# A hybrid diffusion layer on one core: x and positions loaded inside the Fourier stage, its closing barrier split by channel block, and the first choices' rows counted apart

## The reference

```
xl = x + grid_sincos(T, D)
h  = rms_norm(xl, g1) * (1 + scale1) + shift1
y  = sigmoid(g_a) * GLA(h) + sigmoid(g_b) * fourier_mix(h) @ fnet_proj + sigmoid(g_c) * SSD(h)
xl = xl + gate1 * (y @ w_out)
h2 = rms_norm(xl, g2) * (1 + scale2) + shift2
scores = sigmoid(h2 @ router_w)          # 16 experts in 4 groups; best group, then its top 2
xl = xl + gate2 * sum over 2 experts of weight_e * ((silu(h2 @ w1[e]) * (h2 @ w3[e])) @ w2[e])
out = rms_norm(xl, final_g)
```

## Time and profile before

| | us |
|---|---|
| median of 3 runs | 1905.43 (1902.82 to 1907.98) |
| the profiled execution, own time | 1910.72 |
| its span in the profile | 1909.1 |
| PE busy | 1687.8 (88%) |
| DVE busy | 728.6 (38%) |
| ACT busy | 374.4 (20%) |
| POOL busy | 278.9 (15%) |
| mean granted TensorE clock, as a share of full speed | 0.951 |

### The profile page before, as it was taken

One profiled execution on the slowest core, in us unless ns is written; L12 is line 12 of the kernel. 1 busy time (PEld: TensorE's weight loads), 2 busy tenths in 40 slices (PEclk: granted clock), 3 DMA queues, 4 the chain that ended last, 5 costly groups with the idle time before them and its releaser, 6 DMA issues.

```text
span 1909.1 us, 22819 instructions
## 1 busy us (share of the span) xinstructions
PE 1687.8 (88%) x8856; PEld 900.1 (47%) x8857; DVE 728.6 (38%) x1292; ACT 374.4 (20%) x722; POOL 278.9 (15%) x300
## 2 busy tenths in 40 slices
PE   3989799899889889999999999999999867999893
PEld 0554455355355344544454555444656343555441
DVE  1144743754564464620014776214015221222124
ACT  2321232132122122000012333410010121111112
POOL 0003411430530341000000000000000012222122
PEclk9999899999899989999999999999989878999997
DMA  9621101021011116622111001213331645997994
GB/s 314 247 76 44 45 22 45 1 67 44 1 45 45 44 45 220 220 88 89 45 44 44 30 14 45 89 44 104 143 122 45 263 177 205 394 347 291 394 378 152
DMA packets 109537, 242.00 MB, mean 127 GB/s; under 512 B 8505, under 2 KB 18238, under 8 KB 109474
## 3 DMA queue, kind: packets, MB, share of 16 engines
q1 hardware_dynamic: 86800, 180.60, 26.3%
q0 software_dynamic: 14128, 48.51, 7.0%
q10 hardware_dynamic: 8546, 12.03, 1.8%
HBM read 219.10 MB, written 22.02 MB: 126 GB/s over the span
## 4 chain that ended last, share of the span: by engine, by line
PE 75%; DVE 12%; ACT 3%; DMA 3%; issue 3%; POOL 2%; ACTq 2%; DVEq 0%; POOLq 0%; PEldq 0%
PE psum L432 15%; PE psum L1036 8%; PE psum L444 7%; PE psum L722 6%; PE psum L609 4%; PE psum L1058 4%; PE psum L436 4%; PE psum L837 3%; PE psum L667 2%; PE psum L635 2%; PE psum L506 2%; PE psum L454 2%; PE psum L871 1%; PE psum L769 1%; DVE arena L1726 1%
## 5 line engine op out<-in xcount | busy, mean ns | idle before, releaser
L432 PE MATMUL psum<-arena 128*128 128x512 f32 x688 | 312.9, 611 | 10.3 <-issue 4.6
L432 PEld LDWEIGHTS psum<-arena 128*128 128x128 f32 x688 | 132.3, 196 | 171.1 <-issue 163.3
L1036 PE MATMUL psum<-arena 128*32 128x256 f32 x2816 | 166.9, 389 | 1.5 <-DVE arena L2080 1.5
L444 PE MATMUL psum<-arena 128*128 128x512 f32 x352 | 155.2, 600 | 0.1
L609 PE MATMUL psum<-arena 128*128 128x512 f32 x256 | 131.7, 645 | 1.2 <-ACT arena L1230 1.2
L1036 PEld LDWEIGHTS psum<-arena 128*32 128x32 f32 x2816 | 92.2, 111 | 61.2 <-issue 8.5
L722 PE MATMUL psum<-arena 128*128 128x512 f32 x256 | 111.5, 593 | 0.0
L444 PEld LDWEIGHTS psum<-arena 128*128 128x128 f32 x352 | 67.3, 193 | 82.3 <-issue 82.2
L2156 POOL TENSOR_TENSOR arena<-arena 128x512 f32<-128x512 f32 x40 | 49.5, 1248 | 356.5 <-ACT arena L1285 305.6
L2192 POOL TENSOR_TENSOR arena<-arena 128x512 f32<-128x512 f32 x64 | 82.7, 1296 | 101.7 <-ACT arena L1325 101.7
L1682 DVE SCALAR_TENSOR_TENSOR arena<-arena 128x772 f32<-128x772 f32 (+1 forms) x96 | 93.9, 978 | 3.4
(11 more groups left out here) (350 smaller groups left out, 2124.7 us busy)
## 6 DMA issues: line engine op xcount, KB each, us to landing
arena<-exp_w_d SPq DMA_DIRECT2D x48, 2048.0 KB, 17.7
arena<-w_in_d SPq DMA_DIRECT2D x22, 2048.0 KB, 7.9
arena<-ada_w_d POOLq DMA_DIRECT2D x8, 2048.0 KB, 9.1
slots<-arena POOLq DMA_DIRECT2D x1, 9216.0 KB, 27.2
arena<-ada_w_d SPq DMA_DIRECT2D x4, 2048.0 KB, 23.2
arena<-ssd_proj_d SPq DMA_DIRECT2D x4, 2048.0 KB, 9.5
slots<-arena POOLq DMA_DIRECT2D x92, 64.0 KB, 5.0
arena<-slots POOLq DMA_DIRECT2D x22, 256.0 KB, 6.1
```

Source lines behind the costliest of these rows:

```text
L432: ins = mmul(ps[:, 0:T], slot[:, k, m * P:(m + 1) * P], src[:, k, C:NT], start=(k == 0), stop=(k == KD - 1))
L444: ins = mmul(ps[:, 0:n], src[:, k, t * P:(t + 1) * P], slot[:, k, 0:n], start=(k == 0), stop=(k == KD - 1))
L1036: ins = mmul(psU[q * R:(q + 1) * R, 0:2 * HF], XT[:, k % 2, k // 2, :], w13[p][:, :, k, q * HF:(q + 1) * HF], start=(k == 0), stop=(k == K ...
```

## The change

x and the positions are loaded earlier. The positions' transfer stands on ACT's queue at the start of the Fourier stage, into another buffer (`pos2` is now the third matrix of weight set 2), and x's transfer stands behind the last gate eviction of that stage. They have a count each (`pos_in`, `xr_in`). DVE adds the two before its `pb` evictions and also copies out the `g1` and `g2` rows there; PE multiplies these rows right behind the last `fe`, ahead of the wait for the `fe` evictions.

`phase_end(., 4)` is gone on the three engines. DVE's last addition of each block m counts `mT_ready`, and out(0,0) waits for `mT_ready` k + 1 before its product k. SP waits for `mT_ready` 8 in place of `phase_done` before it loads the first expert's weights.

`x_sent` becomes `x_sent0` and `x_sent1`. ACT waits for `x_sent0` alone, loads tile 0 right into `xq` and tile 1 into its place with a transfer each, and counts `xq_ready` without a copy for tile 0. POOL's `fetch_y(0)` waits for `u_full` n in place of `down_full` n.

```diff
-        pos2 = view(phase_base, (TL, D))
+        pos2 = wmem[2][2].rearrange("p (t d) -> p t d", t=TL)
...
                 for k in range(KD):
+                    if made:
+                        pe.wait_ge(S_(made), k + 1)
                     ins = mmul(ps[:, 0:n], src[:, k, t * P:(t + 1) * P], slot[:, k, 0:n],
...
+            for name, c0 in (("g1", 2 * KD), ("g2", 5 * KD)):
...
             for g in range(NG4):
                 pe.wait_ge(*is_free(("fo", g)))
...
-            phase_end(pe, 4)
-
-
-            for name, c0 in (("g1", 2 * KD), ("g2", 5 * KD)):
...
-                project_tok(slot, 512, mT, t, ("wo", j, t), 7)
+                project_tok(slot, 512, mT, t, ("wo", j, t), 7, "mT_ready" if j == 0 and t == 0 else None)
...
-            sp.wait_ge(S_("phase_done"), ENG * 4)
+            sp.wait_ge(S_("mT_ready"), KD)
...
             act.dma_start(rw, a["router_w"].rearrange("(k p) e -> p k e", p=P)).then_inc(S_("rw_in"), 16)
+            act.dma_start(pos2, a["pos"].rearrange("(t p) d -> p t d", p=P)).then_inc(S_("pos_in"), 16)
...
             gates("gb", 4)
+            act.wait_ge(S_("h_folded"), 1)
+            act.dma_start(xr, a["x"][0].rearrange("(t p) d -> p t d", p=P)).then_inc(S_("xr_in"), 16)
...
-            phase_end(act, 4)
-
-
-            act.dma_start(xr, a["x"][0].rearrange("(t p) d -> p t d", p=P)).then_inc(S_("xr_in"), 16)
-            act.dma_start(pos2, a["pos"].rearrange("(t p) d -> p t d", p=P)).then_inc(S_("xr_in"), 16)
+
...
-            act.wait_ge(S_("x_sent"), 16 * 2 * TL)
-            act.dma_start(xrow[:, 0:BATCH * DQ].rearrange("p (i c) -> p i c", c=DQ),
-                          slots[0:BATCH * ROWS_A_TILE, :].rearrange("(i r) (q c) -> (r q) i c", i=BATCH, c=DQ))\
-                .then_inc(S_("xrow_first"), 16)
-            act.wait_ge(S_("xrow_first"), 16)
-            run(xq, xrow[:, 0:DQ], ACT.Copy).then_inc(S_("xq_ready"), 1)
+            act.wait_ge(S_("x_sent0"), 16 * TL)
+            for i, dst in enumerate((xq, xrow[:, DQ:2 * DQ])):
+                act.dma_start(dst, slots[i * ROWS_A_TILE:(i + 1) * ROWS_A_TILE, :].rearrange("r (q c) -> (r q) c", c=DQ))\
+                    .then_inc(S_("xrow_first%d" % i), 16)
+            act.wait_ge(S_("xrow_first0"), 16)
+            act.sem_inc(S_("xq_ready"), 1)
+            act.wait_ge(S_("xrow_first1"), 16)
             act.wait_ge(S_("x_turned"), 1)
             run(xq, xrow[:, DQ:2 * DQ], ACT.Copy).then_inc(S_("xq_ready"), 1)
...
+            dve.wait_ge(S_("xr_in"), 16)
+            dve.wait_ge(S_("pos_in"), 16)
+            step(v.tensor_tensor(xr, xr, pos2, ALU.add))
...
+                v.tensor_tensor(mT[:, m, :], mT[:, m, :], Zg, ALU.add).then_inc(S_("mT_ready"), 1)
+                dve.wait_ge(S_("mT_ready"), m + 1)
...
-            dve.wait_ge(S_("xr_in"), 32)
-            step(v.tensor_tensor(xr, xr, pos2, ALU.add))
...
-                                            yo[:, t, :], None).then_inc(S_("x_sent"), 16)
-            pool.wait_ge(S_("x_sent"), 16 * 2 * TL)
+                                            yo[:, t, :], None).then_inc(S_("x_sent%d" % i), 16)
+            for i in range(2):
+                pool.wait_ge(S_("x_sent%d" % i), 16 * TL)
...
-            pool.wait_ge(S_("down_full"), n)
+            pool.wait_ge(S_("u_full"), n)
```

More of the change, by code:

```diff
@@ L921, in _ @@
                 mmul(o, Ae_mid[0:1, c], ct_mid[0:1, :], start=False, stop=True).then_inc(is_full(key)[0], 1)
+            for name, c0 in (("g1", 2 * KD), ("g2", 5 * KD)):
+                for j in range(2):
+                    key = (name, j)
+                    ps = open_(pe, key)
+                    for i in range(4):
+                        m = c0 + j * 4 + i
+                        ins = mmul(ps[:, i * P:(i + 1) * P], mod[:, m, 0:1].to_broadcast([P, P]), ident,
+                                   start=True, stop=True)
+                    ins.then_inc(is_full(key)[0], 1)
             for g in range(NG4):
@@ L1966, in _ @@
                 dve.wait_ge(*is_free(("g2", j)))
+            for m in range(KD):
+                key = ("pb", m)
+                dve.wait_ge(*is_free(("gb", m)))
+                dve.wait_ge(*is_full(key))
+                ps = bank(key)
+                v.tensor_copy(Zg[:, 0:E1], ps[:, 512:512 + E1]).then_inc(S_("odd_out"), 1)
+                dve.wait_ge(S_("odd_out"), m + 1)
+                step(v.tensor_tensor(Zb[:, 0:E1], ps[:, 0:E1], Zg[:, 0:E1], ALU.add))
+                v.tensor_tensor(Zb[:, T - 1:H:-1], ps[:, 1:H], Zg[:, 1:H], ALU.subtract).then_inc(is_free(key)[0], 1)
+                dve.wait_ge(*is_free(key))
+                step(v.tensor_tensor(Zg, Zb, gateT[:, m, :], ALU.mult))
+                v.tensor_tensor(mT[:, m, :], mT[:, m, :], Zg, ALU.add).then_inc(S_("mT_ready"), 1)
+                dve.wait_ge(S_("mT_ready"), m + 1)
             dve.wait_ge(S_("rw_in"), 16)
```

23 lines of the change are left out of this document (1 added, 22 removed).

## The result

The changed kernel took 1890.98 us in the median of five runs (1884.71 to 1892.52), the kernel before 1906.97 in five runs beside it: 16.0 us less. The ratio on record is 0.990 (0.988 to 0.992); it is an estimate of its own and not the quotient of the medians, and on 1906.97 it comes to 18.7 us (15 to 22). In a later comparison the pair gave 1886.52 and 1909.97, 23.5 less by the medians, with a ratio of 0.988 (0.986 to 0.990), which comes to 22.7.

A forecast was written before the change was run, and what follows sets the result against it. The chain of waits was taken as mostly PE, with winnable gaps at the Fourier stage's end, the experts' start and the tail. 14.7 + 4.8 + 1.5 = 21.0 off the median 1905.43 gave 1884.4 us, range 1876 to 1897.

The forecast's parts named there:

- Part 1: End of the Fourier stage: early x and positions, early gate rows, no barrier; second turn 14.7 us sooner.
- Step a: Gate rows ahead of `pb`: 3.84 us of products fill 0.88 of idle time, so `pb` starts 2.96 later.
- Step b: out(0,0) opens bank 6, still read by DVE for the last `pb`: PE waits 1.5 us.
- Step c: The first turn follows out(0,1) without idle time, the next 7.3 us later: second turn at 1494.2 instead of 1508.93.
- slow restart: Between the first two turns, 10.18 us behind the idle stretch against 7.30 with PE running; the 2.88 would go.
- Part 2: Start of the experts: first choices' scatter counted apart, so PE's first turn comes at 1580.9 instead of 1585.74, 4.8 us gained.
- so 3.4: Tile 0's load beside the scatter's second half: 3.4 us, taken between 2.73 (quiet) and 7.2 (beside weight loads).
- rival C: Tile 0 no sooner than the whole scatter, or tiles 2 and 3 become the wait; Part 2 gives 0 to 1, 1888.7; chance 0.16.
- Part 3: The tail: first choices fetched at `u_full`, 3 us earlier; 1.5 us gained, between 0 and 2.5.
- so each may be quicker by up to 1 or 1.5: In the tail, ACT's send (4.43 us) and the fetch behind it (5.31), with `fetch_y(0)` through 3 us sooner.
- The expert stage passes the gain on: Weight loads follow PE's releases, so all that is gained ahead of the expert stage goes through; no loss there.
- Rival B: Experts bound by weights: earlier gains return as longer weight waits, only Part 3 is left, 1903.9; chance 0.06.

The follow-up runs named there:

- bank0: Changed kernel with out(0,0) opening PSUM bank 0 instead of 6; last `fe` product's end to second turn 59.05 us (60.87 in the changed kernel).
- hold: Changed kernel, POOL issuing the scatter's second four transfers only after the first four landed; last `fe` product to the end 465.39 us (454.87 in the changed kernel).
- p1_only: Changed kernel with scatter, tile loads and tail as in the kernel before; ratio 0.992 to the kernel before, 16 us less.
- best: Changed kernel with the edits of bank0, routes_last and hold, and POOL loading tiles 2 and 3 ahead of its zero-row sends; 1883.21 us, ratio 0.987.
- p2_only: Kernel before with only `x_sent` split and tile 0 loaded right into `xq`, two transfers; ratio 0.998, 4 us less.
- routes_last: Changed kernel with the first two routing products behind the output projection's last parts; last `fe` product to the end 454.76 us (454.87 in the changed kernel).
- after_again: The changed kernel unedited, run again beside best and the kernel before; 1886.52 us, ratio 0.988.
- barrier: Changed kernel with the Fourier stage's closing barrier put back, early loads kept; last `fe` product to second turn 63.89 us (60.87 in the changed kernel).
- x_late: Changed kernel with x issued behind the last `fe` eviction, DVE's addition unmoved; last `fe` product to second turn 67.45 us (60.87 in the changed kernel).

## Why the prediction was right, point by point

- **Part 1, 14.7: measured 15.2.** The mechanism is as forecast, wait for wait. Step a: `pb` starts 3.61 behind F, where it stood 0.88 behind: 2.73 later, forecast 2.96. Step b: 1.58 of bank wait, forecast 1.5, and bank0 shows it is that. Step c: no idle time before the turn and 7.30 to the next, as forecast. The working took the barrier's removal and the early transfers as one; the runs separate them: 1.5 of idle time (in one run 1.6 of clock besides) belongs to the barrier alone, and the other 12 to either. The 2.88 that the forecast calls slow restart was the granted clock: 0.50 from 1500 to 1504 before, 1.00 from 1485 to 1500 after.
- **x's landing: forecast 20.8 from its issue, measured 13.** The 20.8 was that of the positions, which stood behind x; x itself had taken 13.5 in the kernel before. On the safe side, so it cost nothing.
- **Part 2, 4.8: measured 3.8.** ACT's wait ended 4.7 sooner, as forecast (5.1). The term that was mis-sized is "so 3.4" for tile 0's load: it took 5.3, nearer to the 7.2 of the busy row than to the 2.73 of the quiet one. I had interpolated by size, and size is not what decides here: most of the load waits for what POOL had queued ahead (hold: 2.2 without it). It is rival C in part: a first turn 2.6 sooner, not 4.8. The other 1.2 of the 3.8 is luck: PE's first `up` took 5.23 where it had taken 6.50, at a clock of 0.50 for its first 3 us and, before, for its first 6. That is not part 2's doing, nor that of a shorter idle time: p1_only idled for 22.35 and took 5.26, best idled for 12.56 and took 6.53. Put against p1_only, which shares its clock there, the changed kernel's first turn and its turn of tile 2 are both 3.3 sooner; that is the better size of part 2. Tile 2 was not late in the changed kernel, but it was at once in hold, when tile 0 was quicker.
- **Part 3, 1.5: measured 0.1.** `fetch_y(0)` is 3.4 sooner, as forecast. The step that failed is "so each may be quicker by up to 1 or 1.5": the fetch now lies fully in front of ACT's send, which takes 0.8 more, and only the second fetch gains, 0.9. The send's landing hangs on the fetch and not on its own issue: in the changed kernel it lands 10.1 behind the last `down`'s start, and in the seven kernels where ACT issued it 1.0 later it lands at 10.0 to 10.5. Without part 3 (p1_only, p2_only) the tail is as short.
- **The expert stage passes the gain on: right, and 1.7 better than that.** Rival B is refuted: up to the 35th tile nothing changes, and SP issues each of the 39 later loads at the same moment from tile 2's turn, within 0.8. PE does wait for weights at two tiles near the end, 7.3 us before and 6.2 after, but 1.4 of the 1.7 is that the clock did not fall a second time there. No term of the forecast stands for this; it is luck.
- So the right total has a share of luck: 2.4 too much in parts 2 and 3, and 2.7 too little in part 1, ahead of the scatter and in the expert stage. Of the 21.3 some 2.6 are the clock's: 1.2 at the first `up` and 1.4 in the expert stage.

## What to carry to other kernels

The barrier here cost less for the engine that bounds the work (1.5 to 3.0) than for the transfers that stood behind it on an idle engine's queue (12): move the issue or drop the barrier, and look which one the gain needs. When a wait is split so that a small transfer can start sooner, read from the queue rows what will be in flight at that moment; in the changed kernel the small transfer took about as long as the large one ahead of it had left, and in routes_last, where the large one's first half had landed sooner, it took 3.45. Compare profiles from a landmark just ahead of the change, or the clock ahead of it drowns a gain of a few us; and look at the clock in every stretch, since a gain or loss of 1 to 3 us can be the clock's alone.

## What the runs showed of the hardware

**A small transfer on one queue waits for another queue's packets.** 0.26 MB on ACT's queue took 5.3 us beside POOL's scatter, whose packets are 4 KB, at 0.41 MB per us over 16 engines; it took 2.2 without it (hold). The Trainium skill (DMA: Bandwidth & Descriptors, Queues, rings and completion order) says that an engine drains a whole packet of about 9 to 17 descriptors from one ring before it turns to the next; an estimate from that, for descriptors of 4 KB at 0.026 MB per us and engine, is 1.4 to 2.7 us for one such packet. The trace allows it and does not show it: the first packet of ACT's load started 3.5 us behind the issue and 1.0 in hold, 2.5 more, which is within the estimate; but POOL's queue was running out at that moment, so one long packet cannot be told from the rest of the queue. In routes_last the two queues' packets do alternate: ACT's start 1.3 us behind the issue, and half of them have started by 2.9, while POOL's go on beyond 5.5.

**The clock fell beside a busy PE.** Two groups of routing products of 16 columns, 16 instructions each, with a turn between them, stand ahead of out(1,3). In five profiles (before, after, after_again, p1_only, p2_only) out(1,3) then took 7.1; in the seven others with the same order of instructions it took 8.5 to 9.9. PE alone in hold, and the windows around it:

```profile
1519.84 1.85 PE L969 MATMUL psum<-arena 128*128 128x16 f32 x16
1522.02 2.47 PE L969 MATMUL psum<-arena 128*128 128x16 f32 x16
1524.32 9.88 PE L446 MATMUL psum<-arena 128*128 128x512 f32 x16
```

```profile
1520.00:1524.00 4.00, 4.00 (x36) 4.00 (x34) 0.99 (x2) 1.92 (x4) 0.00 (x0) 0.88 0.00 0
1524.00:1528.00 4.00, 4.00 (x8) 1.93 (x8) 0.00 (x0) 0.00 (x0) 0.00 (x0) 0.50 0.00 0
1528.00:1532.00 4.00, 4.00 (x9) 1.76 (x8) 0.00 (x0) 0.00 (x0) 0.00 (x0) 0.76 0.00 0
```

PE is busy for all of these 12 us, and the granted clock is at its lower level, 1.2 GHz, for some 7 of them (it is 0.5 or 1, so 0.88, 0.50 and 0.76 are 1, 4 and 2 us of it); it costs up to 3.4 us, nearly as much as part 2 gains. After, in the same place:

```profile
1530.00:1540.00 10.00, 10.00 (x47) 6.17 (x46) 0.61 (x1) 0.89 (x3) 0.00 (x0) 1.00 0.00 0
```

With both groups put behind it (routes_last, best) out(1,3) was spared, and routing products took the loss. What decides in which run it falls, and whether the routing products have to do with it, was not found.

**The same idle stretch costs the clock in one run and not in another.** Behind 3.04 us of idle time at the barrier the clock stayed at 2.4 GHz in two profiles (before, p2_only) and was at 1.2 GHz for 3.4 us in one (barrier). Behind 4.71 in x_late it was there for 3.4 us, and behind 9.36 in the kernel before it was still there 5.7 us after PE had begun again.
